# Moving the adaLN row dots of a two-layer DiT trunk to other places of the first layer's latent feed-forward loop

## The reference: what is computed

```python
mod = jax.nn.silu(c) @ ada_w[layer] + ada_b[layer]
sh1, sc1, gt1, sh2, sc2, gt2 = jnp.split(mod[:, None, :], N_MOD, axis=-1)

def _conv_ffn(u, w_up, conv_w, w_down):
    gate, val = jnp.split(_dwconv3(u @ w_up, conv_w), 2, axis=-1)
    return (jax.nn.silu(gate) * val) @ w_down
h = h + gt2 * _conv_ffn(_modulate(_rmsnorm(h, norm2[layer]), sh2, sc2), *ffn)
```

## Time and profile before

| | before |
|---|---|
| median of 3 runs | 3197.09 us (3195.32 to 3197.19) |
| the profiled execution | 3190.3 us, its span 3188.5 us |
| PE / DVE / ACT / POOL busy in the whole span | 2957.6 / 2004.6 / 1176.9 / 1240.6 us |
| the loop of the change (605 to 1290 us) | 685 us: PE 658.67, DVE 528.10, ACT 211.32, POOL 455.88 us busy |

### The profile page before, as it was taken

How to read it: one execution, slowest core, us unless ns; L and a number is a source line. 1 busy time by engine, 2 the same in 40 slices (tenths; PEclk the granted TensorE clock), 3 DMA queues, 4 the chain that set the end, 5 groups by cost and what they waited for, 6 DMA issues and landing times. The chain is left out here.

```text
span 3188.5 us, 67120 instructions
## 1 busy us (share of the span) xinstructions
PE 2957.6 (93%) x28494; PEld 2423.1 (76%) x28494; DVE 2004.6 (63%) x2838; ACT 1176.9 (37%) x2200; POOL 1240.6 (39%) x813
## 2 busy tenths in 40 slices
PE   6998999999999999899989888999979799999999
PEld 4655899977777777678867677777867688888887
DVE  4523389678877787702246667777746666666666
ACT  4011155433323323311146566666622433233232
POOL 3212033576667666333211100000004566666664
PEclk9998999999999999899989999999989899999999
DMA  6430045532323332122211011111012112111112
GB/s 238 147 129 34 20 148 177 165 106 87 118 93 99 106 112 86 48 88 84 90 58 53 21 33 31 31 34 32 23 49 83 40 40 67 40 53 66 40 53 79
DMA packets 135913, 247.35 MB, mean 78 GB/s; under 512 B 9537, under 2 KB 97985, under 8 KB 135490
## 3 DMA queue, kind: packets, MB, share of 16 engines
q1 hardware_dynamic: 97314, 193.92, 18.2%
q10 hardware_dynamic: 38304, 49.16, 4.5%
HBM read 221.15 MB, written 21.89 MB: 76 GB/s over the span
## 5 line engine op out<-in xcount | busy, mean ns | idle before, releaser
L1353 POOL TENSOR_TENSOR f_w_lo<-h,f_w_hi 128x512 fp32r<-128x512 f32 x92 | 138.9, 1518 | 150.4 <-ACT f_w_hi L1561 150.4
L3931 POOL TENSOR_TENSOR rw_inv_k<-rw_ss_k,rw_expo 128x4 f32<-128x4 f32 x20 | 20.2, 1008 | 441.1 <-ACT rw_ss_k L4234 441.1
L1429 PE MATMUL ps<-u_hi,f_w_hi 128*128 128x512 f32 x440 | 173.5, 394 | 9.1 <-DVE f_value L1674 4.3
L2209 POOL TENSOR_TENSOR f_w_lo<-f_u_hi_raw,f_w_hi 128x512 fp32r<-128x512 f32 x86 | 129.9, 1521 | 117.4 <-ACT f_w_hi L2457 117.4
L1429 PE MATMUL ps<-u_lo,f_w_hi 128*128 128x512 f32 x440 | 172.8, 393 | 0.0
L1429 PE MATMUL ps<-u_hi,f_w_lo 128*128 128x512 f32 x440 | 172.7, 392 | 0.0
L2209 POOL TENSOR_TENSOR f_w_lo<-f_w_raw,f_w_hi 128x512 fp32r<-128x512 f32 x84 | 127.3, 1523 | 99.1 <-ACT f_w_hi L2457 99.1
L1353 POOL TENSOR_TENSOR f_w_lo<-f_w_raw,f_w_hi 128x512 fp32r<-128x512 f32 x84 | 126.8, 1517 | 96.8 <-ACT f_w_hi L1561 96.8
L167 PE MATMUL ps<-u_hi,w_hi 128*128 128x512 f32 x552 | 145.2, 369 | 6.5 <-ACT cd_stage L1027 6.5
L2240 POOL TENSOR_TENSOR c_lo<-c_raw,c_hi 128x1024 fp32r<-128x1024 f32 x24 | 63.8, 2660 | 217.0 <-ACT c_hi L2419 217.0
L2339 PE MATMUL ps<-u_hi,f_w_hi 128*128 128x512 f32 x352 | 137.8, 391 | 10.4 <-DVE f_value L2591 10.4
(11 more groups left out here) (525 smaller groups left out, 9473.0 us busy)
## 6 DMA issues: line engine op xcount, KB each, us to landing
c_raw<-in_ffn SPq DMA_DIRECT2D x66, 512.0 KB, 3.5
f_w_raw<-in_ffn SPq DMA_DIRECT2D x64, 512.0 KB, 4.2
h<-in_ada_rows ACTq DMA_DIRECT2D x64, 512.0 KB, 3.8
h<-in_ffn SPq DMA_DIRECT2D x34, 512.0 KB, 4.6
f_u_hi_raw<-in_ffn SPq DMA_DIRECT2D x32, 512.0 KB, 4.7
ada_ring_s<-in_ada SPq DMA_DIRECT2D x22, 512.0 KB, 3.3
w_raw<-in_cd_in SPq DMA_DIRECT2D x20, 512.0 KB, 4.2
z_scratch<-cd_stage ACTq DMA_DIRECT2D x15, 640.0 KB, 5.4
```

The costliest lines, as they stand in the source:

```text
L1353: pool.tensor_tensor(two(w_lo[n % RING]), source(x), two(w_hi[n % RING]), ALU.subtract).then_inc(w_split, 1)
L1429: mm = pe.matmul(o, wt, xt, start=t in OPENS and j == 0 and i == 0, stop=j == HK - 1 and i == 2, skip_group_check=t not in OPENS)
L2209: pool.tensor_tensor(two(w_lo[n % RING][:, :]), source(x), two(w_hi[n % RING][:, :]), ALU.subtract).then_inc(w_split, 1)
L3931: pool.tensor_tensor(R.inv[:, :], R.ss[:, :], R.expo[:, :], ALU.pow).then_inc(inv_done, 1)
```

## The change

Before, each of the 32 items (22 up tiles, 10 down steps) holds two dots: an up tile behind U3 and behind C12, a down step behind m = 2 and m = 5. After, an up tile that follows a down step (3, 5, ..., 19) holds one ahead of U2 ("start") and one behind U3, tiles 3, 7, 11 and 15 a third behind C21; the other up tiles hold one behind C12; tile 0 holds three; down steps 0 to 8 hold three, behind m = 0, 3 and 6, and down 9 none. The loads move with them. The number stays 64.

```diff
@@ -2153,10 +2153,40 @@
         s, b = END_BANKS[c][m]
         return K.ps[:, s, b, :]
 
-    def dots_in(kind, n):
-
-        at = sum(2 for x in ITEMS[:ITEMS.index((kind, n))])
-        return at, at + 1
+    def alone(n):
+
+        return n == 0 or (n >= 3 and n % 2 == 1 and n < FT - 1)
+
+    def dot_places(kind, n):
+
+        if kind == "down":
+            return ("m0", "m3", "m6") if n < G - 2 else ()
+        if kind == "end":
+            return ()
+        if not alone(n):
+            return ("C12",)
+        return ("start", "U3") + (("C12",) if n == 0 else ("C21",) if n % 4 == 3 and n < 16 else ())
+
+    DOTS = [x + (place,) for x in ITEMS for place in dot_places(*x)]
+    DOT_NTH = {x: i for i, x in enumerate(DOTS)}
+    assert len(DOTS) == rows.DOTS
+    DOT_LOAD = {"U3": P6, "C21": P5, "m0": 0, "m3": 3, "m6": 5}
+
+    def dots_loaded(kind, n, t):
+
+        found = []
+        for place in dot_places(kind, n):
+            if place == "C12":
+                at = P4 if n == 0 else P6
+            elif place == "start":
+                at = P7 if n == 0 else None
+            else:
+                at = DOT_LOAD[place]
+            if at == t:
+                found.append(DOT_NTH[kind, n, place])
+        if (kind, t) == ("down", KT - 1) and ("up", 2 * n + 3, "start") in DOT_NTH:
+            found.append(DOT_NTH["up", 2 * n + 3, "start"])
+        return found
 
     with nc.Block() as block:
         @block.sync
@@ -2496,11 +2526,13 @@
             def highs_before(step):
                 while highs and free_after(highs[0]) < step:
                     high(highs.pop(0))
-            pending = None
+            pending = due = None
             for i, x in enumerate(STEPS):
                 highs_before(i)
                 kind, n, t = x
-                a, b = dots_in(kind, n)
+                if due is not None:
+                    rows.act_silu(act, due)
+                    due = None
                 if kind == "up":
                     if t == P1 and pending is not None:
                         centre_gate(pending)
@@ -2510,31 +2542,21 @@
                             silu(pending)
                         if n == 0:
                             act.wait_ge(h_out, 16)
-                        rows.act_load(act, a)
-                    if t == P2:
-                        rows.act_silu(act, a)
                     if t == P5:
                         c11(n)
-                    if t == P4:
-                        rows.act_load(act, b)
                     if t == P3:
                         centre_value(n)
-                        rows.act_silu(act, b)
                         pending = n
                 else:
-                    if t == 0:
-                        if pending is not None:
-                            centre_gate(pending)
-                        rows.act_load(act, a)
+                    if t == 0 and pending is not None:
+                        centre_gate(pending)
                     if t == 2:
                         if pending is not None:
                             silu(pending)
-                        rows.act_silu(act, a)
                         pending = None
-                    if t == 3:
-                        rows.act_load(act, b)
-                    if t == 4:
-                        rows.act_silu(act, b)
+                for i in dots_loaded(kind, n, t):
+                    rows.act_load(act, i)
+                    due = i
             highs_before(len(STEPS))
             assert not highs
             nxt.act(act)
@@ -2636,38 +2658,38 @@
                 c_add(m)
             pending = None
             for kind, n in ITEMS:
+                def dot(place):
+                    if (kind, n, place) in DOT_NTH:
+                        rows.dve_dot(dve, DOT_NTH[kind, n, place])
                 if kind == "up":
-                    a, b = dots_in(kind, n)
                     if pending is not None:
                         gated(pending)
                         rounded(pending)
+                    dot("start")
                     merge(n, U2)
                     merge(n, U3)
                     if pending is not None:
                         low(pending)
-                    rows.dve_dot(dve, a)
+                    dot("U3")
                     merge(n, C22)
                     merge(n, C21)
+                    dot("C21")
                     taps(n, 1)
                     merge(n, C12)
-                    rows.dve_dot(dve, b)
+                    dot("C12")
                     taps(n, 0)
                     pending = n
                 elif kind == "down":
-                    a, b = dots_in(kind, n)
                     late = n < G - 2
                     for m in range(KT):
                         add(n, m)
+                        dot(f"m{m}")
                         if m == 1:
                             gated(pending)
                         if m == (7 if late else 1):
                             rounded(pending)
                         if m == (7 if late else 2):
                             low(pending)
-                        if m == 2:
-                            rows.dve_dot(dve, a)
-                        if m == 5:
-                            rows.dve_dot(dve, b)
                     pending = None
                 else:
                     rows.dve_finish(dve)
```

## The result

| | before | after |
|---|---|---|
| median, same chip | 3197.02 us (6 runs) | 3212.62 us (6 runs, 3199.16 to 3217.78) |
| ratio, 95% interval | | 1.0044 [1.0025, 1.0062] |
| the loop, P7 of tile 0 to the first product behind it | 688.5 us | 703.9 us |

A forecast was written before the change was run, and what follows sets the result against it. PE, busy 93% of the span, was taken as the bound, its waits set by a chain starting on POOL. Eight groups +24.8, tile 0 +3.2 and tiles 19 to 21 +0.5 us gave +28.5: 3225.6 us, range 3196 to 3243.

The forecast's parts named there:

- Removed: Dots taken from C12 of tiles 3 to 19 (0.38 us off the chain) and U3 of paired tiles (0.82 us PE wait gone).
- The first rival: POOL is not held up, only DVE's own order counts: faster by 8.7 us, 3188.4 us; chance 0.15.
- the second: Rival: only the sure part holds, casts on time, clock mostly up: +6.4 us, 3203.5 us, reaching 3201 to 3210; chance 0.14.
- The sum: Adds all terms: groups +2.5 or +3.7 us, eight groups +24.8, tile 0 +3.2, tiles 19 to 21 +0.5: +28.5 us.
- start dot, through POOL: Head of tiles after a down step: the dot ahead of U2 makes POOL's S2 0.77 us later.
- late casts: Head of the tile after a down step: casts wait behind a load held by dot m6; 0.9 us taken, up to 1.85.
- taps meet POOL once more: Tiles after a down step: the late taps meet POOL again, costing 0.4 us, between 0 and 1.2.
- P4 of the paired tile later: P4 of the paired tile comes 1.7 us later, making PE's wait 2.6 us.
- Added behind C21: Tiles 3, 7, 11, 15: the dot delays S2 or the taps by 1.2 us, bounds 0 and 1.25.
- the clock: Behind PE's longer wait in each group the granted clock drops, costing 1.66 us.
- Tile 0 to P1 of tile 3: Tile 0's P3 comes 5.1 us late, tile 1 gives back a 1.9 us C22 wait: +3.2 us in all.
- Tile 19 to the end: Tiles 19 to 21 cost +0.5 us, chosen between -2 and +1.5; down 9 changes nothing.

The follow-up runs named there:

- e2: Kernel e1 with the dots ahead of U2 of tiles 3 to 19 put back behind C12 and U3's load back at P7; 3186.71 us, ratio 0.9991.
- e10: Kernel e8 with down steps 0 to 8 holding one dot fewer and tiles 3 to 19 (odd) a start dot whose load comes early; 3190.23 us, ratio 0.9993.
- e4: Changed kernel with full dots in place but only the first and 49th piece loaded, so no dot or cast waits for loads; 3191.52 us, ratio 1.0011.
- e7: Changed kernel with the start dot's load issued behind the next tile's two casts, not ahead of them; 3198.09 us, ratio 1.0023.
- e1: Changed kernel without the four C21 dots, made behind C12 of tile 19 and in down 9 instead; 3202.42 us, ratio 1.0037.
- e9: Kernel e8 with the second dot of tiles 3, 5, ..., 19 behind C21 instead of C12; 3198.4 us, ratio 1.0026.
- e11: Changed kernel run again without an edit, on another chip; 3205.74 us, ratio 1.0045.
- e5: Changed kernel with tile 0's dots behind U3 and C12 as before the change, its third dot in down 9; 3204.81 us, ratio 1.0042.
- e6: Changed kernel with only the start dots of tiles 3 to 19 cut to 8 of 1024 columns, same loads and order; 3194.1 us, ratio 1.001.
- e8: Kernel before with U3's dots of paired tiles 4 to 20 moved into down steps, three each, tile 0's silu also moved; 3188.01 us, ratio 0.9992.

## Why the prediction had the path right and the size wrong

**Right: the chain.** POOL's S2, ACT's cast, `centre_value`, the taps, silu, U3, P4 is late in every group, by POOL being held up and by casts that stand behind a load that waits for a dot. The C22 waits went, as "Removed" said, and the C12 dot was worth 0.34 us (0.38 said). A half-clock stretch costs 1.58 us (1.66 said), dot m6 does wait on its load, and P3 of tile 0 comes 4.3 us later behind P7 (5.1 said). The first rival (POOL not held up) falls with e2 and e10; the second, with waits of 1.5 us and a clock that stays up, is e10 but not the change. Two signs that the prediction named for itself were only half met: S2 in tile 3 ends 0.86 us later behind P1 and not 1 us or more, and the waits over 2.3 us with half clock behind them are found in some tiles only.

**Wrong: the sizes in "The sum",** nearly all on the same side.

| term, per group | said | measured | shown by |
|---|---|---|---|
| start dot, through POOL | 0.77 | 0.4 to 0.5 | e10, e4: `centre_value` at 17.67 and 17.78 |
| late casts | 0.9 | 0.9 to 1.1, once 1.9; 0.4 to 0.5 ahead of the C21 tiles | the table above; 0 in e7 |
| taps meet POOL once more | 0.4 | 0 | from `centre_value` to taps over, with a C12 dot, it is 11.98 us both late (e10; e1, tile 19) and on time (before) |
| C12 dot gone | -0.38 | -0.34 | the same without a C12 dot: 11.64 us |
| P4 of the paired tile later | 1.7 | 0.9 to 1.1, once 1.9 | P4 behind P1 of the odd tile: 34.6 to 34.8 and 35.6 us, before 33.7 |
| C21 dot | 1.2 | 1.0; late by its load 2.2 | e4, e9, e11 |
| P4 with a C21 dot | 2.9 | 1.4 to 1.7; in e11 1.8 to 3.1 | 35.1 to 35.4 us; 35.5 to 36.9 |

The step that failed first is the one where the prediction held a rule against a row and took the rule: "0.77 us by the rule and 0.55 by the row". The start dot makes POOL's three subtractions take 4.79 us, and three take 3.8 when nothing holds them (a step is 1.24 us in the earlier trace rows, the last takes 1.29), so POOL loses 1.0 us, the 0.99 of the earlier trace rows, and not the dot's 1.21. Less the gap of 0.44 that is 0.55, and 0.4 to 0.5 arrived. The 0.4 us for the taps' meeting POOL once more were added to this, and nothing of them came. Together these two terms are 0.7 to 0.8 us too much in each of the eight groups.
The Trainium skill (SBUF — State Buffer, "SBUF: two separate sides") has the loser blocked for the whole instruction. The trace agrees that DVE and POOL take turns; the length that was lost is nearer to the row.

The second is in "Added behind C21": 1.2 us was added on top of casts 0.9 late. In the first profile the dot costs 1.0 and the casts ahead of just these tiles are only 0.4 to 0.5 late. That was the luck of this profile. In all 45 groups of the five profiles that have the start dot's load ahead of the casts (after, e1, e5, e6, e11) the casts start 1.92 or 1.93 us behind the start of dot m6, and m6 follows m0 by two loads: the lateness of the casts is that of dot m0. In 21 of the groups the paired tile ahead had no stretch at half clock, and the casts are 0.8 to 2.2 us late. In 24 it had one, which holds PE back against DVE (in the kernel after, the C12 dot of the paired tile starts 19.6 us or more ahead of the next P1, and 18.1 without it): 14 of these are 0.36 to 0.54 late, and the other ten, where dot m0 waited 0.34 us or more for its load, 0.8 to 1.9. So a stretch at half clock gives back about 0.6 us in the next group. In e11 tiles 11 and 15, which hold a C21 dot, have casts 1.0 us late, and tiles 9, 13 and 19, which hold none, 0.4 to 0.5.

The third is the clock. The sum gave all eight groups a stretch, 13.3 us. In the groups of tiles 4 to 18 there are six behind the eight waits, and both of the profiled waits that differ only in this are 2.31 us long; in e11 there are five.

**The three stretches of the sum.** The eight groups (P1 of tile 3 to P1 of tile 19) grew by 12.1 us and not by 24.8. The waits in them grew by 3.5 us, where +11.8 was said: no wait ahead of P4 is over 2.31 us here, and the eight ahead of P3, 0.8 us each, went. Six stretches at half clock are 9.5 us. Together that is 13.0; for each wait for C22 that went 0.16 us comes off (P4 took 2.99 us with such a wait behind it and 2.83 without).

**Tile 0 to P1 of tile 3** was said to cost +3.2 and costs +5.1 us. P3 of tile 0 needs no wait, since P4 was itself 2.7 us late and partly at half clock. What was missed: the waits ahead of P4 in tiles 1 and 2 grew from 2.06 and 2.28 to 2.61 and 2.60, and two of 0.6 us for `keep` came in. The prediction put nothing for the silu that moved ahead of a cast; e5, e8, e9 and e10 have 2.5 to 3.0 us of this with tile 0's dots as before. **Tile 19 to the end** was said to cost +0.5 and gave 1.8 back.

So 12.1 + 5.1 - 1.8 = 15.4 us. Counted the other way, PE's waits in the loop grew by 4.8 us (28.1 to 32.9, the last one ahead of the phase behind included), and seven more stretches at half clock are 11.1: 15.9. About two thirds of the loss is thus the clock in this profile, and a third is waiting. In e11 it is 6.8 us of waits and six stretches, 9.5 us.

In parts shown by edits, one after the other: all of the change but the start and C21 dots gains 5.0 us (e2), the start dots with their loads lose 17.2 (e1 against e2), the C21 dots lose 3.3 (after against e1); that is the 15.4. In the eight groups alone the same steps are -8.3, +14.2 and +6.2 us, which is the 12.1. Waits and clock are both in each, and each is the difference of single executions.

## What to carry to other kernels

Work put "under" a wait of its own engine is free only if it holds up no other engine then and no queue has its load in front of something urgent: here the dot was hidden on DVE and paid for on POOL (0.4 us) and on ACT (0.4 to 1.9 us). With one buffer, a load issued right behind the last user puts the whole of the landing time in front of what follows in the issuing queue; issue it behind the urgent instructions (e7), or free the buffer a slot earlier (e10). And making one long wait of two short ones can lose at the clock what it won in idle time: 0.92 + 0.82 us cost less than one of 2.3 with 1.58 us of slower matmuls behind it. Last, an instruction that happens once can be the one that was moved: the silu in tile 0 went along with the loads, and the cast behind it is almost 4 us late in e8.
